# Norm and decay rows of the next block's mixer issued in the out-projection stage of the block before

## Chip, cores and metric

The kernel runs on the eight cores of one Trainium2 chip. Every core runs the same program on one of the eight sequences of the batch, with no exchange between cores. Time is the device time of the slowest core, in microseconds. A core has five instruction streams that run side by side and wait for each other through semaphores: TensorE (PE), VectorE (DVE), ScalarE (ACT), GpSimd (POOL), and SyncE (SP), which here only issues DMAs. Each takes its instructions strictly in order, so an instruction that waits holds up all that stand behind it on its engine.

## What is computed

A Mamba-2 layer and a sliding-window attention layer, each followed by a gated convolutional FFN. The part that the change moves is the start of the Mamba mixer: the normed input `h`, the step sizes `dt`, and what follows from them alone, the running log decay `a_cum` and its exponentials.

```python
h = rms_norm(x, a_norm)
z, xBC, dt = jnp.split(h @ in_proj, [SSM_INNER, SSM_INNER + SSM_CONV_DIM], axis=-1)
xBC = jax.nn.silu(causal_dwconv(xBC, conv_w, conv_b))
dt = jax.nn.softplus(dt + dt_bias);  A = -jnp.exp(A_log)
a = dt * A;  a_cum = jnp.cumsum(a, axis=chunk_position)
seg = a_cum[l] - a_cum[s]                      # decay = exp(seg), causal
y_diag = einsum(cb * decay, x * dt);  states = einsum(B, exp(a_cum[-1] - a_cum), x * dt)
y_off = einsum(C, previous state) * exp(a_cum);  chunk_decay = exp(a_cum[-1])
y = group_rms_norm((y + x * D) * silu(z));     x = x + y @ out_proj
x = x + conv_ffn(x);   x = x + attention(x);   x = x + conv_ffn(x)
```

## The kernel before

The 2048 tokens are cut into four blocks of 512 (b = 0 to 3). Per block there are generators of steps: `mixer_steps(b)`, `mixer_out(b)`, `ffn_steps(b, l)` and `attn_steps(b)`. Each returns a list of (cost, function). `weave` merges lists by the share of their own total cost that each has done, and `FL.run` (lines 1639 to 1647) calls the functions in that order. They run in this sequence:

```python
    FL.run(mixer_steps(0))
    FL.run(mixer_out(0))
    for b in range(NBLK - 1):
        front = ffn_steps(b - 1, 1) if b >= 1 else []
        FL.run(weave(front + ffn_steps(b, 0), mixer_steps(b + 1)))
        FL.run(weave(attn_steps(b), mixer_out(b + 1)))
```

The texts below call the first line M0, the second O0, and the two lines in the loop A1, B1 (b = 0), A2, B2 (b = 1) and A3, B3 (b = 2). In an A stage the FFN of one block shares the engines with the mixer of the next; in a B stage attention of one block shares them with the out-projection of the next.

Calling a function does not emit at once. It records operations; `schedule` (line 432) then places each on its engine. It walks time with a planned cost for each operation and always takes, among those that would be ready, the one recorded first (line 476). A switch of ScalarE's function table weighs 300 places in that choice (line 472). So the order of recording is a priority, not the order of execution: an operation recorded late can be placed early if its inputs and its buffers are free.

`mixer_steps(b)` begins with what the change moves:

- four steps `nrm(t)` of 128 tokens. `tnorm` (line 858) does on ScalarE Square with a row sum, Ln, Exp, and the scaled copy into `sb_Cs`, then eight transposes on TensorE, and on VectorE the product with the gain into `sb_hM`. Its input is `sb_xR` for block 1, and `sb_macc` (filled by a DMA) for blocks 2 and 3. The FFN norms are the same code with `sb_facc` or `sb_fsq` in place of `sb_Cs`, and `sb_hF` in place of `sb_hM`.
- `dt1` (line 938): eight matmuls of 96 output rows with `sb_hM`, then Exp, Ln and the decay scan into `sb_mln`, the write `er_scr` to DRAM and its read `fetch(0)` into `sb_Er`, the Exp and products that make `sb_xtok`, and then the sixteen small float32 matmuls on `sb_cf` with `sb_xtok` and `sb_mln`, whose result VectorE copies to `sb_tokS`.
- `dt3` (line 987): each of two rows is split in three bfloat16 parts on VectorE, written to `al_scr` and `as_scr`, and read back by `rows(0)` as twelve small DMAs into `sb_SR` and `sb_SL`. The segment matmuls (line 366, `sb_SR,sb_SL`) of group 0 need them.
- `dt2` (line 1028): one matmul on `sb_tokS`, then Exp into `sb_cdec`.

After that come eight groups: `inproj(g)` (six chains of eight matmuls with `sb_hM`; conv on ScalarE and VectorE) woven with `ssd(g - 1)`. `fetch` and `rows` are also called by `ssd` for the next group. The weights come through two rings of five slots, `sb_ring_mw` (mixer) and `sb_ring_fw` (FFN, attention). `mixer_out(b)` (line 1229) multiplies `sb_ybuf` by the out-projection: 128 matmuls, in TensorE rows `sb_ring_mw,sb_ybuf`. In O0 it takes turns over all eight banks of PSUM, in B stages over banks 0 and 1.

## Time and profile before

| | |
|---|---|
| median of three runs | 2025.77 us (2016.21, 2025.77, 2180.25) |
| the profiled execution | 2015.09 us; span of its slowest core 2014.0 us |
| spans of the eight cores | 1987.5 to 2014.0 us |
| TensorE matmul busy | 1826.7 us (91%) |
| VectorE, ScalarE busy | 1388.5 us (69%), 1197.6 us (59%) |
| chain that ended last | TensorE 70%, DMA 13%, issue 6%, DVE 5%, ACT 5% |

The table is for core 6, the slowest. The chain is followed back from the last instruction: at each step to what released it. TensorE's matmul time on it says how long the kernel is at least with this order and this clock; what can be taken away lies in the 9% in which TensorE does nothing. The granted clock, averaged over the span, was between 0.975 and 0.981 of full speed on the eight cores. M0 lasts until about 200 us and O0 until 229 us; A1 runs to about 505, B1 to 620, A2 to about 990, B2 to 1100, A3 to about 1465, B3 to about 1580.

### The profile page before, as it was taken

What the parts mean: (1) busy time and instruction counts of PE and PEld (TensorE: products, weight loads), DVE (VectorE), ACT (ScalarE), POOL (GpSimd) and SP (SyncE); (2) the same over time, 40 slices, a digit from 0 to 9 for tenths busy, and PEclk for the clock granted to TensorE, in tenths of its full rate; (3) what the DMA queues carried; (4) which work ended last, traced back from release to release, by engine and by line L of the source; (5) the groups of instructions that cost most, each with busy time, mean ns of one, the idle gap of its engine ahead of it and who ended that gap; (6) DMA issues with size and microseconds to landing.
All of it is one profiled execution on the core that took longest, in us unless ns stands there. A gap on an engine that the chain in (4) does not pass through costs nothing.

```text
span 2014.0 us, 34053 instructions; the slowest of 8 cores (1987.5 to 2014.0 us)
## 1 busy us (share of the span) xinstructions
PE 1826.7 (91%) x9831; PEld 824.7 (41%) x10024; DVE 1388.5 (69%) x2384; ACT 1197.6 (59%) x2144; POOL 259.5 (13%) x434
## 2 busy tenths in 40 slices
PE   4878798999898999899899998899988898999999
PEld 2333443434434444444433443444443344433344
DVE  5898587887757766687675875688676665774362
ACT  3899665756765664565677564576476643665340
POOL 1222111212121111111211111000102000020000
PEclk9999999999898999999999999999999999999999
DMA  7785698999546769999984999944422443433344
GB/s 149 142 169 106 136 196 174 187 181 207 106 130 134 156 142 198 247 227 228 225 233 93 236 222 216 302 160 143 143 83 105 133 153 118 147 115 105 126 148 145
DMA packets 111062, 330.59 MB, mean 164 GB/s; under 512 B 14752, under 2 KB 33312, under 8 KB 110880
## 3 DMA queue, kind: packets, MB, share of 16 engines
q0 software_dynamic: 31392, 113.65, 35.5%
q1 hardware_dynamic: 79488, 214.74, 32.2%
q8 instruction: 86, 1.41, 0.3%
q14 instruction: 96, 0.79, 0.1%
HBM read 375.60 MB, written 66.39 MB: 219 GB/s over the span
## 4 chain that ended last, share of the span: by engine, by line
PE 70%; DMA 13%; issue 6%; DVE 5%; ACT 5%; SPq 0%; POOL 0%; DVEq 0%; ACTq 0%; POOLq 0%
PE ps_ps L353 63%; PE ps_ps L366 5%; DMA w<-sb_ring_fw 4%; DMA sb_ring_fw<-w 2%; DMA sb_ring_mw<-w 2%; PE ps_ps L373 2%; DMA out<-sb_xR 1%; ACT sb_facc L391 1%; DMA sb_Er<-er_scr 1%; DMA sb_xR<-x 1%; DVE sb_macc L417 1%; DMA sb_facc<-pos 1%; ACT sb_macc L391 1%; DVE sb_uF L406 1%; DVE sb_facc L417 1%
## 5 line engine op out<-in xcount | busy, mean ns | idle before, releaser
L353 PE MATMUL ps_ps<-sb_hF,sb_ring_fw 128*128 128x512 bf16 x2394 | 569.4, 381 | 9.9 <-DVE sb_facc L417 2.6
L353 PE MATMUL ps_ps<-sb_hM,sb_ring_mw 128*128 128x512 bf16 (+1 forms) x1525 | 392.3, 393 | 23.5 <-DVE sb_macc L417 10.2
L353 PE MATMUL ps_ps<-sb_ring_fw,sb_uF 128*128 128x512 bf16 (+1 forms) x1650 | 391.3, 376 | 15.9 <-DMA sb_ring_fw<-w 5.6
L353 PEld LDWEIGHTS ps_ps<-sb_hF,sb_ring_fw 128*128 128x128 bf16 x2464 | 235.3, 98 | 281.5 <-issue 21.2
L417 DVE SCALAR_TENSOR_TENSOR sb_facc<-ps_ps,sb_cst,sb_facc 128x511 f32<-128x511 f32 (+2 forms) x400 | 295.6, 744 | 19.2 <-PE ps_ps L353 2.5
L417 DVE SCALAR_TENSOR_TENSOR sb_macc<-ps_ps,sb_cst,sb_macc 128x511 f32<-128x511 f32 (+1 forms) x336 | 248.1, 744 | 13.8 <-DVE sb_facc L406 0.7
L391 ACT ACTIVATE sb_facc<-ps_ps,sb_cst 128x512 f32<-128x512 f32 x213 | 162.6, 766 | 154.8 <-PE ps_ps L353 142.1
L353 PEld LDWEIGHTS ps_ps<-sb_ring_fw,sb_uF 128*128 128x128 bf16 x1696 | 157.6, 98 | 207.4 <-issue 48.9
L353 PEld LDWEIGHTS ps_ps<-sb_hM,sb_ring_mw 128*128 128x128 bf16 (+1 forms) x1568 | 151.7, 101 | 200.9 <-issue 50.1
L406 DVE TENSOR_TENSOR sb_xR<-sb_xR,ps_ps 128x512 f32<-128x512 f32 x128 | 86.3, 683 | 117.2 <-PE ps_ps L353 115.6
L429 POOL DMA_DIRECT2D sb_ring_fw<-w x152 | 83.3, 548 | 634.8 <-PE ps_ps L353 538.6
L406 DVE TENSOR_TENSOR sb_uF<-sb_uF,ps_ps 128x512 bf16<-128x512 bf16 x176 | 118.1, 681 | 68.1 <-PE ps_ps L353 42.6
L353 PE MATMUL ps_ps<-sb_ring_mw,sb_ybuf 128*128 128x512 bf16 (+1 forms) x593 | 148.5, 377 | 7.6 <-DMA sb_ring_mw<-w 2.7
L391 ACT ACTIVATE sb_macc<-ps_ps,sb_cst 128x512 f32<-128x512 f32 x119 | 91.6, 770 | 106.6 <-PE ps_ps L353 99.9
L391 ACT ACTIVATE sb_prevB<-sb_prevF 128x256 bf16<-128x256 f32 x128 | 52.7, 412 | 134.2 <-PE ps_ps L353 49.7
L398 ACT ACTIVATE sb_uF<-sb_facc 128x512 bf16<-128x512 f32 x176 | 96.7, 618 | 24.9 <-DVE sb_facc L417 21.6
L406 POOL TENSOR_TENSOR sb_stmp<-sb_prevF,sb_cdec 128x256 f32<-128x256 f32 x112 | 72.3, 646 | 274.3 <-DVE sb_prevF L406 217.4
L406 DVE TENSOR_TENSOR sb_prevF<-sb_stmp,ps_ps 128x256 f32<-128x256 f32 x112 | 46.5, 415 | 75.8 <-PE ps_ps L353 51.3
L353 PEld LDWEIGHTS ps_ps<-sb_ring_mw,sb_ybuf 128*128 128x128 bf16 x608 | 56.0, 98 | 79.4 <-issue 27.6
L398 ACT ACT_TABLE_LOAD x50 | 64.2, 1283 | 37.7 <-DVE sb_facc L417 24.9
L391 ACT ACT_TABLE_LOAD x54 | 69.3, 1283 | 24.3 <-PE ps_ps L366 16.7
L353 PE MATMUL ps_ps<-sb_hM,sb_ring_fw 128*128 128x512 bf16 x345 | 77.5, 385 | 2.0 <-DVE sb_hM L406 1.6
(219 smaller groups left out, 2315.7 us busy)
## 6 DMA issues: line engine op xcount, KB each, us to landing
sb_ring_fw<-w POOLq DMA_DIRECT2D x152, 512.0 KB, 10.0
sb_ring_fw<-w SPq DMA_DIRECT2D x142, 512.0 KB, 3.6
w<-sb_ring_fw SPq DMA_DIRECT2D x76, 512.0 KB, 14.1
sb_ring_mw<-w SPq DMA_DIRECT2D x74, 512.0 KB, 6.1
sb_ring_mw<-w POOLq DMA_DIRECT2D x64, 512.0 KB, 8.7
w<-sb_ring_mw SPq DMA_DIRECT2D x32, 512.0 KB, 9.4
sb_Er<-er_scr SPq DMA_DIRECT2D x28, 512.0 KB, 11.6
sb_xR<-x SPq DMA_DIRECT2D x16, 512.0 KB, 10.1
```

Source lines behind the costliest of these rows:

```text
L353: return self.add("pe", lambda e: e.matmul(out, lhsT, rhs, start=start, stop=stop), [lhsT, rhs] + ([] if start else [out]), [out], cost=ma ...
L366: ins = e.matmul(out, lhsT, rhs, start=start, stop=stop)
L373: return self.add("pe", lambda e: e.transpose(out, in_, ident), [in_, ident], [out], cost=250.0 if _f32(in_) else 80.0)
L391: return self.add("act", lambda e: e.activation(out, in_, func, **kw), rd, wr, cost=c, tab=TABLE.get(func, 0))
L398: ins = e.activation(out, in_, func)
L406: return self.add(eng, lambda e: e.tensor_tensor(out, in0, in1, op), [in0, in1], [out], cost=c)
L417: return self.add("dve", lambda e: e.scalar_tensor_tensor(out, in0, scalar, in1, op0, op1), rd, [out], cost=190.0 + 1.1 * _n(out))
L429: return self.add(queue, lambda e: e.dma_start(out=out, in_=in_), [in_], [out], dma_sem=sem, cost=900.0 if queue == "pool" else 60.0, lat= ...
```

## The change

The four norm steps, `dt1`, `dt3` and `dt2` leave `mixer_steps` and become a function of their own, `mixer_pre(b, b_in)`. `dt3` follows straight on `dt1` now. For block 0 it runs alone ahead of `mixer_steps(0)`. For block 1 it is woven with `mixer_out(0)`: the transposes and small matmuls use PSUM banks 6 and 7, and the out-projection takes turns over banks 0 to 5 in place of all eight. For blocks 2 and 3 it stands at the end of the list of `mixer_out(1)` and `mixer_out(2)`, on banks 0 and 1, so that it is woven with the last part of attention. `fetch` and `rows` take the block as an argument and do the same as before.

```diff
-    def mixer_steps(b):
+    def mixer_pre(b, b_in):
+
         t0 = b * TB
...
-            bk = b_x() if solo else b_in()
+            bk = b_in()
...
-            fetch(0)
+            fetch(b, 0)
...
-            rows(0)
+            rows(b, 0)
...
         def dt2():
-            bk = b_x() if solo else yb
+            bk = b_in()
...
+        S.append((300.0, dt3))
+        S.append((300.0, dt2))
+        return S
+
+    def mixer_steps(b):
+        t0 = b * TB
+        solo = (b == 0)
...
-                S += weave(inproj(g), ([(1.0, dt3)] if g == 0 else []) + [(800.0, lambda: None)] + side)
+                S += weave(inproj(g), [(800.0, lambda: None)] + side)
...
-        bo = Banks(list(range(8)) if solo else [0, 1])
+        bo = Banks(list(range(6)) if solo else [0, 1])
...
-        return S
+        if solo:
+            return weave(S, mixer_pre(1, Banks([6, 7])))
+        return S + (mixer_pre(b + 1, bo) if b + 1 < NBLK else [])
...
+    FL.run(mixer_pre(0, Banks([0, 1, 2, 3, 4, 5])))
     FL.run(mixer_steps(0))
     FL.run(mixer_out(0))
```

The recorded operations are the same in number and kind; the order on the engines is not. On TensorE, at the end of O0 and the start of A1, the order before was this (`sb_cm` rows are the transposes, with `sb_Cs` those of the mixer's norm, with `sb_facc` and `sb_fsq` those of the FFN's; the 96x512 row is `dt1`):

```order
L353 MATMUL ps_ps<-sb_ring_mw,sb_ybuf 128x512 x66
L373 MATMUL ps_ps<-sb_cm,sb_Cs 128x128 x8
L373 MATMUL ps_ps<-sb_cm,sb_facc 128x128 x8
L373 MATMUL ps_ps<-sb_cm,sb_Cs 128x128 x8
L373 MATMUL ps_ps<-sb_cm,sb_fsq 128x128 x8
L373 MATMUL ps_ps<-sb_cm,sb_Cs 128x128 x8
L373 MATMUL ps_ps<-sb_cm,sb_facc 128x128 x8
L373 MATMUL ps_ps<-sb_cm,sb_Cs 128x128 x8
L373 MATMUL ps_ps<-sb_cm,sb_fsq 128x128 x8
L353 MATMUL ps_ps<-sb_hM,sb_ring_mw 96x512 x8
L353 MATMUL ps_ps<-sb_hF,sb_ring_fw 128x512 x8
```

In the changed kernel the mixer's transposes, `dt1` and the sixteen small matmuls stand ahead, among the out-projection's matmuls; from the last of these small ones on, TensorE has:

```order
L353 MATMUL ps_ps<-sb_cf,sb_mln 128x32
L353 MATMUL ps_ps<-sb_ring_mw,sb_ybuf 128x512 x5
L353 MATMUL ps_ps<-sb_tokS,sb_cf 128x128
L353 MATMUL ps_ps<-sb_hM,sb_ring_mw 128x512 x8
L373 MATMUL ps_ps<-sb_cm,sb_facc 128x128 x8
L373 MATMUL ps_ps<-sb_cm,sb_fsq 128x128 x8
L353 MATMUL ps_ps<-sb_hM,sb_ring_mw 128x512 x8
L373 MATMUL ps_ps<-sb_cm,sb_facc 128x128 x8
L373 MATMUL ps_ps<-sb_cm,sb_fsq 128x128 x8
L353 MATMUL ps_ps<-sb_hM,sb_ring_mw 128x512 x6
L353 MATMUL ps_ps<-sb_hF,sb_ring_fw 128x512 x8
```

So 22 matmuls of the mixer's in-projection (8, 8 and 6) now stand between the last out-projection matmul and the FFN's first, where there were none, and the mixer's 32 transposes and `dt1` are gone from that place.

At the end of B2, still on TensorE, the order before was this (`sb_ring_fw,sb_uF` rows are here attention's output projection, `sb_fsq` the transposes of the FFN's norm that hangs on it):

```order
L373 MATMUL ps_ps<-sb_cm,sb_Cs 128x128 x13
L353 MATMUL ps_ps<-sb_ring_fw,sb_uF 128x512 x12
L373 MATMUL ps_ps<-sb_cm,sb_Cs 128x128 x16
L353 MATMUL ps_ps<-sb_hM,sb_ring_mw 96x512 x2
L373 MATMUL ps_ps<-sb_cm,sb_fsq 128x128 x8
L353 MATMUL ps_ps<-sb_hM,sb_ring_mw 96x512 x6
L353 MATMUL ps_ps<-sb_hF,sb_ring_fw 128x512 x40
L353 MATMUL ps_ps<-sb_hM,sb_ring_mw 128x512 x8
L353 MATMUL ps_ps<-sb_hF,sb_ring_fw 128x512 x2
L353 MATMUL ps_ps<-sb_cf,sb_xtok 128x32
```

And now:

```order
L353 MATMUL ps_ps<-sb_hM,sb_ring_mw 96x512 x3
L353 MATMUL ps_ps<-sb_ring_fw,sb_uF 128x512 x12
L353 MATMUL ps_ps<-sb_cf,sb_xtok 128x32
...
L353 MATMUL ps_ps<-sb_cf,sb_mln 128x32
L353 MATMUL ps_ps<-sb_tokS,sb_cf 128x128
L353 MATMUL ps_ps<-sb_hM,sb_ring_mw 128x512 x4
L373 MATMUL ps_ps<-sb_cm,sb_fsq 128x128 x8
L353 MATMUL ps_ps<-sb_hM,sb_ring_mw 128x512 x12
L353 MATMUL ps_ps<-sb_hF,sb_ring_fw 128x512 x40
```

The small matmuls on `sb_xtok` stood 50 large matmuls behind `dt1`; now they stand 12 behind it, and ahead of the transposes on which the FFN's matmuls hang. At the end of B1 they moved in the same way: eight matmuls of the mixer's first chain and twelve of attention's output stood between, now thirteen of the latter with one attention unit and one set of transposes.

Near the start of the program, on VectorE, one pair changed places. Before:

```order
L421 CAST sb_CBb<-sb_Cs 96x512
L421 CAST sb_Btok<-sb_Wt 96x512
L417 SCALAR_TENSOR_TENSOR sb_CBb<-sb_CBb,sb_cst,sb_Cs 96x512
L421 COPY sb_tokS<-ps_ps 128x256
L417 SCALAR_TENSOR_TENSOR sb_Cs<-sb_Btok,sb_cst,sb_Wt 96x512
```

And now:

```order
L421 CAST sb_CBb<-sb_Cs 96x512
L421 CAST sb_Btok<-sb_Wt 96x512
L421 COPY sb_tokS<-ps_ps 128x256
L417 SCALAR_TENSOR_TENSOR sb_CBb<-sb_CBb,sb_cst,sb_Cs 96x512
L417 SCALAR_TENSOR_TENSOR sb_Cs<-sb_Btok,sb_cst,sb_Wt 96x512
```

The copy to `sb_tokS`, which waits for TensorE's sixteen small matmuls, now stands ahead of the operation that completes `sb_CBb`, which the DMA to `al_scr` takes. Both built programs have 1728 ScalarE operations with a function; where the table that they need changes from one to the next, the order before has 104 switches, and the order now 110: 24 in place of 22 in A2, 26 in place of 22 in A3, and as many as before elsewhere.

## Rows read from the trace of the kernel before

**Rows 1.** The page, busy time of engines: engine, us (share of the span), instructions.
```profile
PE 1826.7 (91%) x9831; PEld 824.7 (41%) x10024; DVE 1388.5 (69%) x2384; ACT 1197.6 (59%) x2144; POOL 259.5 (13%) x434
```

**Rows 2.** Busy time by stretch: stretch, length, engines' busy us, PE clock, DMA share, GB/s.
```profile
75.00:100.00 25.00, 19.78 (x149) 9.63 (x152) 23.82 (x45) 23.24 (x43) 6.80 (x11) 1.00 0.70 120
650.00:675.00 25.00, 24.90 (x119) 11.49 (x119) 18.51 (x33) 15.23 (x30) 3.31 (x6) 1.00 0.84 169
```

**Rows 3.** Timeline of TensorE from the end of O0: start, length, instruction, [idle before].
```profile
223.66 5.34 PE L353 MATMUL ps_ps<-sb_ring_mw,sb_ybuf 128*128 128x512 bf16 x23 [0.17 <-DMA sb_ring_mw<-w]
...
230.76 0.61 PE L373 MATMUL ps_ps<-sb_cm,sb_fsq 128*128 128x128 bf16 x8
234.46 0.61 PE L373 MATMUL ps_ps<-sb_cm,sb_Cs 128*128 128x128 bf16 x8 [3.08 <-ACT sb_Cs L391]
...
239.30 1.01 PE L373 MATMUL ps_ps<-sb_cm,sb_Cs 128*128 128x128 bf16 x8 [3.19 <-ACT sb_Cs L391]
...
241.79 2.66 PE L353 MATMUL ps_ps<-sb_hM,sb_ring_mw 128*96 128x512 bf16 x8 [0.44 <-DVE sb_hM L406]
244.50 1.67 PE L353 MATMUL ps_ps<-sb_hF,sb_ring_fw 128*128 128x512 bf16 x7
```

**Rows 4.** Timeline, same stretch: VectorE's last FFN norm product, ScalarE's part of a conv.
```profile
241.56 1.21 DVE L406 TENSOR_TENSOR sb_hF<-ps_ps,sb_cst 128x1024 bf16<-128x1024 bf16 x1
...
246.27 0.78 ACT L391 ACTIVATE sb_facc<-ps_ps,sb_cst 128x512 f32<-128x512 f32 x1 [0.32 <-PE ps_ps L353]
```

**Rows 5.** TensorE's sixteen small matmuls in A1, first and last of eight rows.
```profile
250.97 0.30 PE L353 MATMUL ps_ps<-sb_cf,sb_xtok 96*128 96x32 f32 x2
...
252.46 0.39 PE L353 MATMUL ps_ps<-sb_cf,sb_mln 96*128 96x32 f32 x2
```

**Rows 6.** Timeline of all engines near the start of the program.
```profile
32.13 0.68 ACT L391 ACTIVATE sb_mln<-ps_ps,sb_cst 96x512 f32<-96x512 f32 x1 [8.05 <-PE ps_ps L353]
...
38.66 0.61 PE L353 MATMUL ps_ps<-sb_cf,sb_xtok 96*128 96x32 f32 x2 [4.25 <-DVE sb_xtok L406]
...
39.11 0.74 DVE L417 SCALAR_TENSOR_TENSOR sb_CBb<-sb_CBb,sb_cst,sb_Cs 96x512 bf16<-96x512 bf16 x1
...
39.92 0.31 SPq L429 DMA_DIRECT2D al_scr<-sb_CBb  x1
...
42.37 0.42 DVE L421 COPY sb_tokS<-ps_ps 128x256 f32<-128x256 f32 x1 [2.52 <-PE ps_ps L353]
...
46.91 3.65 SPq L429 DMA_DIRECT2D sb_SR<-al_scr  x8
...
52.74 3.26 SPq L429 DMA_DIRECT2D sb_SL<-as_scr  x4
...
65.12 0.62 PE L366 MATMUL ps_ps<-sb_SR,sb_SL 47*128 47x512 bf16 x4 [3.43 <-DMA sb_SL<-as_scr]
```

**Rows 7.** Timeline of TensorE and VectorE at the end of B1.
```profile
610.62 1.24 PE L353 MATMUL ps_ps<-sb_hM,sb_ring_mw 128*96 128x512 bf16 x5
...
620.11 1.01 PE L373 MATMUL ps_ps<-sb_cm,sb_fsq 128*128 128x128 bf16 x8 [3.37 <-ACT sb_fsq L391]
...
620.38 0.68 DVE L406 TENSOR_TENSOR sb_xtok<-sb_xtok,sb_Wt 96x512 f32<-96x512 f32 x1
```

**Rows 8.** Timeline of TensorE at the end of B2.
```profile
1096.63 0.61 PE L373 MATMUL ps_ps<-sb_cm,sb_Cs 128*128 128x128 bf16 x8 [0.48 <-ACT sb_Cs L391]
1097.67 0.61 PE L373 MATMUL ps_ps<-sb_cm,sb_Cs 128*128 128x128 bf16 x8 [0.43 <-ACT sb_Cs L391]
1099.84 0.83 PE L353 MATMUL ps_ps<-sb_hM,sb_ring_mw 128*96 128x512 bf16 x2 [1.57 <-DVE sb_hM L406]
```

**Rows 9.** A DMA of A1 and what waited for it: issue on SP, then TensorE.
```profile
322.04 0.41 SPq L429 DMA_DIRECT2D sb_Er<-er_scr  x1
...
341.41 0.59 PE L353 MATMUL ps_ps<-sb_BCb 128*128 128x128 bf16 x4 [7.91 <-DVE sb_prevF L406]
```

**Rows 10.** The page, groups of ScalarE's table loads: count, busy us, mean ns, idle before.
```profile
L391 ACT ACT_TABLE_LOAD x54 | 69.3, 1283 | 24.3 <-PE ps_ps L366 16.7
```

More of the change, by code:

```diff
@@ L978, in toks @@
             def toks():
-                bk = b_x() if solo else b_in()
+                bk = b_in()
                 for t in range(4):
@@ L1124, in post @@
                     if q2 == 1 and g < 7:
-                        fetch(g + 1)
-                        rows(g + 1)
+                        fetch(b, g + 1)
+                        rows(b, g + 1)
                 h["w", q2] = later(1, post)
@@ L1197, in mixer_steps @@
             side = ssd(g - 1) if g >= 1 else []
-            if g == 0:
-                side = [(300.0, dt2)]
             if g >= 2:
```

60 lines of the change are left out of this document (31 added, 29 removed).

## The prediction

> **What bounds the kernel now.** I read the page first: TensorE is busy for 1826.7 of 2014.0 us [rows 1]. At most the rest, 187 us, can be won, and the start of the program, before the first norm is ready, has a good part of it. Then I read the busy time by stretch, which shows two regimes. In M0 VectorE and ScalarE are full (23.82 and 23.24 of 25 us) and TensorE waits for them. In an A stage TensorE is full (24.90 of 25) and ScalarE has room (15.23 of 25) [rows 2]. So a norm that is moved out of an A stage gives nothing where TensorE is full; it gives something only at a boundary between stages. For these I read the timeline.
>
> At the boundary of O0 and A1 the last run of out-projection matmuls ends at 223.66 + 5.34 = 229.00, and the FFN's first matmul starts at 244.50. TensorE waits 3.08 and 3.19 us for ScalarE there, which norms two tiles at a time, one of the mixer and one of the FFN: a pair takes 239.30 - 234.46 = 4.84 us [rows 3]. This is the hole that the change can fill. The ends of B1 and B2 look otherwise. The waits are 3.37 us [rows 7] and 0.48 + 0.43 + 1.57 = 2.48 us [rows 8], and the mixer's norm already lies among attention's last steps there: `schedule` took it early although it was recorded late.
>
> **The change part by part.** No operation is added or removed, so the sum is one of waits.
>
> *O0 and A1.* Into O0 go four sets of transposes (0.61 us each, 2.4), `dt1`'s eight matmuls (at 5.34 / 23 = 0.23 us each, 1.9) [rows 3], and the sixteen small ones with `dt2`'s (252.46 + 0.39 - 250.97 = 1.9 [rows 5], and I add 0.2). The 66 out-projection matmuls stood without a gap, so O0 ends 6.4 us later. Behind it the FFN's last two tiles follow the first two by one ScalarE cycle: the first two's transposes start until 230.76, the next come 4.84 us later, at 235.6, and with 0.61 for them and 1.21 for VectorE's product [rows 3, 4] `sb_hF` is whole at 237.4, 8.4 us after the last out-projection matmul. Two conv operations of ScalarE (0.78 each [rows 4]) now come between, so I take 9.5. The FFN starts at 229.0 + 6.4 + 9.5 = 244.9 in place of 244.50, 0.4 later. But by then 22 in-projection matmuls (5.1 us) and the small ones (2.1) are done, which before came behind 244.50. Net: 7.2 - 0.4 = 6.8 us gained. Bounds: if TensorE waited for nothing there, it would need only the 64 transposes (eight sets at 0.61, 4.9) and `dt1` (1.9) of the 15.5 us, so at most 8.7 are won; if the ScalarE operations of `dt1` (0.68 for the first [rows 6], about five such) still stand ahead of the FFN's norms, 3.4 of it goes: at least 3.4.
>
> *The start.* VectorE's copy to `sb_tokS` waits for TensorE and now stands ahead of the operation that completes `sb_CBb`. That one runs at 42.37 + 0.42 in place of 39.11, 3.7 us later, and so does the DMA to `al_scr` (39.92). SP issued `al_scr`'s reads 7.0 us after the write, at 46.91, and needs 3.65 us for the eight; now it starts at about 50.6 and ends at 54.3, and the four `sb_SL` reads behind them, issued at 52.74, wait until then: 1.5 us late. TensorE already waits 3.43 us for them at 65.12 [rows 6]. M0 runs behind VectorE and ScalarE, which need these matmuls' result, so nothing covers it: 1.5 us lost. Bounds 0 (the order of the conv work around it absorbs it) and 3.7.
>
> *B1 and A2.* The sixteen small matmuls need `sb_xtok`, the end of a chain through ScalarE and VectorE. At the start of the program, with both engines free, it took 38.66 - 32.13 = 6.5 us from `dt1`'s end [rows 6]; at the end of B1, between attention's operations, 620.38 + 0.68 - (610.62 + 1.24) = 9.2 us [rows 7]. I take 8. Behind `dt1` there now stand 13 large matmuls (3.0), one attention unit (0.8) and a set of transposes (0.6): TensorE waits 8 - 4.4 = 3.6 us. Then `dt2`'s matmul waits for the copy (0.42 [rows 6] and the handovers, 0.7), and the FFN's first matmul for the product behind the last transposes (1.21 [rows 4] and a handover, 1.5); two chains of the in-projection stand between and cover the norm. That is 5.8 us in place of 3.37 and some 0.8 of small gaps: 1.6 lost. The out-projection's matmuls now end seven matmuls earlier in attention's list, 1.6 us of TensorE work that no longer fills attention's gaps; I count a fourth of it. Together 2 us lost. Bounds: 3.4 gained, if only the old wait goes and no new one comes, and 6 lost.
>
> *B2 and A3.* Here only the 12 matmuls of attention's output (2.8 us) lie between `dt1` and the small ones. With one more attention operation on ScalarE than at the start the chain takes 7.8: a wait of 5.0, and 0.7 for the copy, against 2.48 before and 0.7 of small gaps. 2.5 lost. The out-projection ends four attention units earlier, 14 matmuls or 3.2 us of cover; half of it, 1.6. Together 4 us lost. Bounds: 3.2 gained, 8 lost. The early small matmuls used to stand 50 matmuls behind `dt1`, where 11.6 us of work hid the chain; this cover is what is gone.
>
> *Table loads.* The order has six more of them, four in A3 and two in A2, each 1.283 us [rows 10], 7.7 us of ScalarE. Both stages leave it 10 of 25 us free [rows 2], so 0 by the row, at most 7.7. The Trainium skill, in ScalarE: Activation LUTs, "Table sets: the hidden batching unit", asks to batch activations by table set; by that rule, taking a block of Exp and Ln out of a stage full of Silu should save loads. The trace agrees on the price of one, and the built order speaks against the saving: 110 switches, not fewer than 104.
>
> *What the DMAs do.* In A1 the whole core stood for 7.91 us behind one `sb_Er` read that was issued at 322.04 and landed about 18 us later [rows 9]. Such a wait depends on what else is queued in that moment. The change shuffles it without aim: 0, bounds 8 either way.
>
> Sum: -6.8 + 1.5 + 2 + 4 = +0.7 us on 2015.1, so 2015.8. This execution is the fastest of the comparable ones; with the 2016.21 and 2025.77 of the table the mean is 2019.0, 3.9 above it. I put the same on the sum: 2019.7.
>
> **The rivals.**
>
> *A, the waits cancel.* Above: 2019.7. For it speaks that at B1 and B2 the norms had already been taken early, so that there the change does little of what it says, and that where it does, TensorE meets a new wait in line.
>
> *B, all boundaries gain.* In-projection matmuls are ready when an A stage starts and fill every hole: 8.7 at A1, the old waits of 3.4 and 3.2 at A2 and A3, nothing lost at the start, and half the `sb_Er` wait (4): 19 us, so 2000. Against it: the small matmuls stand ahead of that filler at A2 and A3, and TensorE can't pass them.
>
> *C, the blocked line costs more.* The wait for `sb_xtok` also delays the FFN norm behind it. ScalarE has to do `dt1`'s chain, and in B1 the Exp of `dt2` too, before the last norm, so that the two waits add instead of overlapping, and TensorE's clock falls: `dt1`'s eight matmuls took 2.66 us (0.33 each) behind the waits of A1, against 0.23 before them [rows 3]. With the upper bounds of both ends (6 + 8), 3.7 at the start and 3.4 at A1: +14, so 2034. It decides from the point where `sb_xtok` is ready more than 10 us after `dt1` in both stages.
>
> *D, ScalarE carries the loads.* [...] As a mechanism here: each of the six loads delays the Silu whose product TensorE needs next, 7.7 us: 2027.4. Only 0.61 of ScalarE's time is taken in A2, which speaks against it.
>
> **How the numbers follow.** A 0.45, B 0.26, C 0.21, D 0.06, something else 0.02. The prediction is A's. Its own range is 2009 to 2030 (the sum's bounds, less the chance that they all fall to one side, and the 10 us by which comparable executions differ). From B to C the range is 1998 to 2040; it leaves out about 2 in 10. A measurement of this kernel can tell about 2%, 40 us, from no change. No case here reaches that: B would need twice its gain, C thrice its loss. Faster by over 2%: 0.01; within 2%: 0.96; slower by over 2%: 0.03.
>
> **What would show it.** In the profile after: between the last out-projection matmul of O0 and the FFN's first, 22 matmuls on `sb_hM` and no wait over 3 us; the `al_scr` write at about 43.5 and the first segment matmuls at about 66.6; a wait for `sb_xtok` of 3 to 5 us ahead of the small matmuls at the end of B1 and of 4 to 6 at the end of B2; 110 table loads. If the waits at `sb_xtok` are under 1 us, B is right. If A1's `sb_Er` wait, or a new one like it, comes or goes by 8 us or more, the sum is wrong for a reason that it doesn't hold.

## The result, and the profile after the change

| | before | after |
|---|---|---|
| median, slowest core | 2020.18 us (14 runs) | 2034.01 us (14 runs) |
| ratio after to before | | 1.0066, 95% interval 1.0047 to 1.0085 |
| profiled execution, span | 2015.09, 2014.0 us | 2026.11, 2025.0 us |
| mean of the eight cores' spans over all comparable runs | 2005.1 us (111 runs) | 2016.0 us (10 runs) |

The change costs 0.66%, 13 us on the slowest core and 11 us on an average core. (The medians are over all 14 runs; the ratio, the last row and everything below leave out the runs in which one half of the chip ran at a lower clock, five of before's and four of after's.) The last row of the table is the finer measure: every run lists the span of each core, the slowest of eight is a matter of luck by some us, and the mean over eight is less so. The text calls it the mean of spans. Its difference is 10.9 ± 2.6 us (95%, as all intervals below). Before's 111 runs are those of the experiments below, on five chips with means of 2004.2 to 2007.0 us, and none ran beside after's ten, which adds a us or two of doubt.

The page after the change (core 1, the slowest), busy time of engines, and the groups of ScalarE's table loads, as [rows 1, 10]:

```profile
PE 1843.3 (91%) x10024; PEld 823.8 (41%) x10024; DVE 1384.8 (68%) x2384; ACT 1208.8 (60%) x2150; POOL 264.8 (13%) x434
...
L391 ACT ACT_TABLE_LOAD x58 | 74.4, 1283 | 25.1 <-PE ps_ps L366 17.0
...
L398 ACT ACT_TABLE_LOAD x52 | 66.7, 1283 | 31.8 <-PE ps_ps L353 18.3
```

Six more instructions on ScalarE, and 58 + 52 = 110 table loads. TensorE's busy times can't be compared between the pages: x9831 before and x10024 now are the same matmuls, with fewer records missing. The two regimes of [rows 2] are as they were, 23.70 and 23.93 us of VectorE and ScalarE in M0, TensorE full in A2:

```profile
75.00:100.00 25.00, 19.59 (x145) 9.18 (x145) 23.70 (x46) 23.93 (x43) 6.17 (x10) 1.00 0.80 142
650.00:675.00 25.00, 25.00 (x126) 11.50 (x124) 20.14 (x37) 12.65 (x26) 2.64 (x5) 1.00 0.89 174
```

**O0 and A1.** TensorE's timeline, as [rows 3]: start, length, instruction, [idle before].

```profile
231.89 0.39 PE L353 MATMUL ps_ps<-sb_tokS,sb_cf 128*128 128x128 f32 x2
232.11 1.89 PE L353 MATMUL ps_ps<-sb_hM,sb_ring_mw 128*128 128x512 bf16 x8
...
236.65 1.89 PE L353 MATMUL ps_ps<-sb_hM,sb_ring_mw 128*128 128x512 bf16 x8 [1.75 <-DVE sb_xR L406]
238.99 0.61 PE L373 MATMUL ps_ps<-sb_cm,sb_facc 128*128 128x128 bf16 x8 [0.45 <-ACT sb_facc L391]
241.18 0.61 PE L373 MATMUL ps_ps<-sb_cm,sb_fsq 128*128 128x128 bf16 x8 [1.59 <-ACT sb_fsq L391]
242.69 1.46 PE L353 MATMUL ps_ps<-sb_hM,sb_ring_mw 128*128 128x512 bf16 x6 [0.91 <-DVE sb_macc L417]
243.98 1.89 PE L353 MATMUL ps_ps<-sb_hF,sb_ring_fw 128*128 128x512 bf16 x8
```

The 22 matmuls on `sb_hM` are there, no wait is over 2 us, and the four waits sum to 4.70 where [rows 3] had 3.08 and 3.19 beside smaller ones. The wait of 1.75 for `sb_xR` comes from the moved steps themselves: VectorE ran the products of `dt3` from 231.75 to 235.9 without a gap, ahead of the `sb_xR` sum at 235.83.

**The start**, all engines, as [rows 6]:

```profile
38.86 0.61 PE L353 MATMUL ps_ps<-sb_cf,sb_xtok 96*128 96x32 f32 x2 [4.90 <-DVE sb_xtok L406]
...
42.56 0.42 DVE L421 COPY sb_tokS<-ps_ps 128x256 f32<-128x256 f32 x1 [3.17 <-PE ps_ps L353]
43.08 0.75 DVE L417 SCALAR_TENSOR_TENSOR sb_CBb<-sb_CBb,sb_cst,sb_Cs 96x512 bf16<-96x512 bf16 x1
...
43.90 0.31 SPq L429 DMA_DIRECT2D al_scr<-sb_CBb  x1
...
48.23 4.08 SPq L429 DMA_DIRECT2D sb_SR<-al_scr  x8
...
52.47 3.27 SPq L429 DMA_DIRECT2D sb_SL<-as_scr  x4
...
61.97 0.39 PE L366 MATMUL ps_ps<-sb_SR,sb_SL 47*128 47x512 bf16 x2
```

The write to `al_scr` is 4.0 us later than before, but its reads are issued 4.3 us behind it in place of 7.0, and the `sb_SL` reads at 52.47, where they were.

**The end of B1**, TensorE, as [rows 7]. The small matmuls wait for nothing; the FFN's transposes and first matmul do:

```profile
615.72 0.61 PE L373 MATMUL ps_ps<-sb_cm,sb_facc 128*128 128x128 bf16 x8 [1.18 <-ACT sb_facc L391]
617.99 2.10 PE L353 MATMUL ps_ps<-sb_ring_fw,sb_uF 128*128 128x512 bf16 x9 [1.66 <-DVE sb_hF L406]
619.93 0.30 PE L353 MATMUL ps_ps<-sb_cf,sb_xtok 96*128 96x32 f32 x2
...
627.81 0.61 PE L373 MATMUL ps_ps<-sb_cm,sb_fsq 128*128 128x128 bf16 x8 [1.39 <-ACT sb_fsq L391]
630.00 10.14 PE L353 MATMUL ps_ps<-sb_hF,sb_ring_fw 128*128 128x512 bf16 x40 [1.58 <-DVE sb_hF L406]
```

**The end of B2**, TensorE, as [rows 8], then four stretches of it by engine (stretch, length, busy of PE, PEld, DVE, ACT, POOL, clock, DMA share, GB/s):

```profile
1100.82 0.38 PE L366 MATMUL ps_ps<-sb_cm 64*128 64x512 bf16 x2
1102.88 0.41 PE L366 MATMUL ps_ps<-sb_facc,sb_vtok 128*64 128x512 bf16 x2 [1.69 <-DVE sb_uF L406]
...
1112.77 2.37 PE L353 MATMUL ps_ps<-sb_ring_fw,sb_uF 128*128 128x512 bf16 x8 [2.80 <-DVE sb_uF L406]
1116.67 0.60 PE L353 MATMUL ps_ps<-sb_cf,sb_xtok 96*128 96x32 f32 x2 [1.54 <-DVE sb_xtok L406]
...
1120.94 0.77 PE L353 MATMUL ps_ps<-sb_tokS,sb_cf 128*128 128x128 f32 x2 [0.68 <-DVE sb_tokS L421]
...
1126.76 8.80 PE L353 MATMUL ps_ps<-sb_hF,sb_ring_fw 128*128 128x512 bf16 x40
```

```profile
1091.00:1106.00 15.00, 12.46 (x104) 5.53 (x100) 10.08 (x12) 14.39 (x24) 0.57 (x1) 1.00 0.34 129
1091.00:1101.00 10.00, 9.59 (x80) 4.12 (x76) 7.49 (x10) 9.39 (x15) 0.00 (x0) 1.00 0.50 191
1101.00:1111.00 10.00, 6.41 (x42) 2.75 (x40) 4.79 (x6) 7.04 (x15) 1.05 (x2) 1.00 0.48 53
1111.00:1126.00 15.00, 11.02 (x47) 7.18 (x48) 11.08 (x21) 7.57 (x17) 2.29 (x4) 0.66 0.96 206
```

TensorE waits more for `sb_uF`, the late products of attention, than for `sb_xtok`. In the last 15 us the granted clock is 0.66 on average, between the levels of 1.2 and 2.4 GHz, behind 10 us in which TensorE was busy for 6.41. The sixteen small matmuls take 3.6 us (1116.67 to 1120.94 - 0.68), where [rows 5] has 1.9. Before has such a fall at this place too, but a shorter one: between the out-projection's end and 12 us into A3 TensorE was busy for 2.9 us per core at the lower level, and in after for 8.9. A matmul takes twice as long there, so this costs 4.5 us in place of 1.5. ScalarE shows why attention is late:

```profile
1101.43 1.04 ACT L391 ACTIVATE sb_facc<-sb_xR 128x1024 bf16<-128x1024 f32 x1
...
1103.16 1.13 ACT L391 ACTIVATE sb_Cs<-sb_macc,sb_nss 128x1024 bf16<-128x1024 f32 x1
1104.20 1.14 ACT L391 ACTIVATE sb_facc<-sb_xR,sb_nss 128x1024 bf16<-128x1024 f32 x1
1105.24 1.00 ACT L391 ACTIVATE sb_facc<-ps_ps 128x1024 bf16<-128x1024 f32 x1
1109.20 0.69 ACT L391 ACTIVATE sb_mln<-ps_ps,sb_cst 96x512 f32<-96x512 f32 x1 [2.96 <-PE ps_ps L353]
1109.79 0.62 ACT L391 ACTIVATE sb_facc<-sb_facc 128x512 f32<-128x512 f32 x1
```

The last scores of attention are ready at 1101.2 (`sb_cm`, 1100.82 + 0.38), and their Exp, `sb_facc<-ps_ps`, runs at 1105.24: ScalarE first does a norm of the FFN (`sb_xR`) and the last of the mixer's (`sb_Cs`). Over the eight cores this delay is 4.0 us, and 1.4 in before, where these norms come later. `dt1`'s Exp (`sb_mln`) stands ahead of attention's two `sb_facc<-sb_facc` as well, but its idle 2.96 us cost attention little: their input, VectorE's sum with `sb_esink`, is itself ready only at 1109.20 (1108.51 + 0.69), so they come 0.6 us later by the Exp, and the second one another 0.5 by the Ln behind it. e4 below has attention's operation ahead of `dt1`'s Exp and still 4.0 us of waits for `sb_uF` per core, against 4.9 here. Nor is it that ScalarE is full: 14.39 of 15 us here, and before has a stretch with 14.2.

**Stage by stage.** From the timelines of all eight cores I took the times of the same marks, and subtracted the TensorE work ahead of each in the built order (0.213 us for a matmul of 512 columns, the cost that the steps' lists use), so that work done earlier or later doesn't count. Mean of eight cores, us more than before; the standard error (not the 95% interval) is 1.6 to 2.1 in M0, 0.3 to 0.9 at the boundaries, 1.4 to 2.8 in the A stages. Counting the small float32 matmuls at their measured 0.11 us and setting the end marks of the A stages otherwise moves the boundary rows by up to 0.9 us at A1 and A3 and up to 2 at A2. The stretch behind A3 has no row.

| | after | e1 | e2 | e3 | e4 | e7 | e15 |
|---|---|---|---|---|---|---|---|
| M0, to its last state matmul | +6.2 | +5.9 | +3.3 | +2.1 | +2.2 | +1.1 | +3.8 |
| to the FFN's first matmul in A1 | -3.6 | +0.8 | -3.1 | +0.1 | +0.1 | 0.0 | -3.3 |
| rest of A1 | 0.0 | +3.7 | +5.1 | +0.3 | +3.0 | +4.4 | -5.1 |
| B1, to the first in A2 | +1.0 | +0.8 | +0.4 | +1.0 | +0.2 | +2.5 | +0.7 |
| rest of A2 | -1.9 | +1.9 | +1.6 | -2.4 | +0.2 | +1.5 | +1.0 |
| B2, to the first in A3 | +10.4 | +0.4 | -0.6 | +1.7 | +6.4 | -0.6 | -0.9 |
| rest of A3 | -2.7 | +1.2 | -0.3 | -0.4 | -4.0 | +6.5 | +0.5 |
| whole execution | +8.2 | +14.6 | +6.6 | +4.5 | +8.7 | +14.8 | -2.0 |

The profiled execution of before is a short one: its mean of spans is 1999.9, 5.2 below the mean of its runs. So every column has some 5 us too much, in M0 and A1 (e2, e3, e4 and e7 have M0 in before's order and still show +1.1 to +3.3; e1, e3, e4 and e7 have A1 in before's order and show +0.3 to +4.4). Totals are therefore taken from the runs, and of this table only the boundaries.

For M0 the kept traces give a better comparison. Eleven kernels have VectorE's order of before up to the end of O0, and two, after and e1, have the new one. The new ones reach their first segment matmul 0.2 us sooner, at 155 us they are level, and their last state matmul comes 4.4 us later, at 209.5 in place of 205.1; the standard errors are 0.5 to 0.6. So M0's loss appears in its last 50 us, and not at the start.

### The profile page after: what moved, and what is told of

Read it like the earlier page. It is cut to its first block, busy times and chain, and to the rows that moved or that the text cites. A ratio compares the mean times of both kernels' runs of the same rounds, so it can differ in the third digit from the quotient of the medians.

```text
span 2025.0 us, 34178 instructions; the slowest of 8 cores (1990.6 to 2025.0 us)
## 1 busy us (share of the span) xinstructions
PE 1843.3 (91%) x10024; PEld 823.8 (41%) x10024; DVE 1384.8 (68%) x2384; ACT 1208.8 (60%) x2150; POOL 264.8 (13%) x434
## 4 chain that ended last, share of the span: by engine, by line
PE 70%; DMA 13%; ACT 6%; issue 5%; DVE 5%; POOL 0%; SPq 0%; DVEq 0%; ACTq 0%; POOLq 0%
PE ps_ps L353 63%; PE ps_ps L366 5%; DMA w<-sb_ring_fw 4%; DMA sb_ring_fw<-w 3%; PE ps_ps L373 2%; DMA sb_Er<-er_scr 2%; ACT sb_facc L391 1%; DMA sb_facc<-pos 1%; DMA sb_xR<-x 1%; DMA out<-sb_xR 1%; DVE sb_uF L406 1%; DVE sb_macc L417 1%; DMA sb_ring_mw<-w 1%; DVE sb_facc L417 1%; ACT sb_macc L391 1%
## 5 line engine op out<-in xcount | busy, mean ns | idle before, releaser
L353 PE MATMUL ps_ps<-sb_hF,sb_ring_fw 128*128 128x512 bf16 x2464 | 577.5, 382 | 4.2 <-DVE sb_hF L406 2.9
L353 PE MATMUL ps_ps<-sb_hM,sb_ring_mw 128*128 128x512 bf16 (+1 forms) x1568 | 391.0, 386 | 26.6 <-DVE sb_macc L417 11.9
L353 PE MATMUL ps_ps<-sb_ring_fw,sb_uF 128*128 128x512 bf16 (+1 forms) x1696 | 395.4, 377 | 18.8 <-DVE sb_uF L406 8.8
## 6 DMA issues: line engine op xcount, KB each, us to landing
sb_ring_fw<-w POOLq DMA_DIRECT2D x152, 512.0 KB, 10.4
sb_xR<-x SPq DMA_DIRECT2D x16, 512.0 KB, 11.4
```

Source lines behind the costliest of these rows:

```text
L353: return self.add("pe", lambda e: e.matmul(out, lhsT, rhs, start=start, stop=stop), [lhsT, rhs] + ([] if start else [out]), [out], cost=ma ...
```

## The experiments

All are against the runs of before on the same chip. The table gives the ratio on the slowest core with its 95% interval, and the difference in the mean of spans with a 95% interval. The expectations quote such differences against all runs of before that there were by then, so theirs differ from the table's by some tenths of a us.

| | ratio, slowest core | mean of spans, us |
|---|---|---|
| e1 block 0 alone | 1.0043 (1.0023, 1.0064) | +5.7 ± 2.9 |
| e2 block 1 alone | 1.0013 (0.9995, 1.0032) | -0.1 ± 2.0 |
| e3 block 2 alone | 1.0045 (1.0026, 1.0064) | +2.1 ± 2.7 |
| e4 block 3 alone | 1.0022 (0.9998, 1.0047) | +3.7 ± 2.2 |
| e5 e1, banks of before | 0.9996 (0.9979, 1.0013) | -0.3 ± 2.7 |
| e6 e4, split | 1.0016 (0.9998, 1.0035) | +4.0 ± 2.4 |
| e7 e4, appended | 1.0044 (1.0027, 1.0061) | +8.9 ± 2.1 |
| e8 whole change, banks as e5 | 1.0046 (1.0029, 1.0063) | +7.7 ± 2.1 |
| e9 before, `sb_Er` on ScalarE's queue | 1.0007 (0.9991, 1.0023) | +2.2 ± 1.6 |
| e10 e2, same | 0.9994 (0.9978, 1.0010) | -0.8 ± 2.5 |
| e11 e7, late rows | 1.0024 (1.0007, 1.0042) | +4.2 ± 2.2 |
| e12 e11, paced | 1.0017 (1.0002, 1.0032) | +1.0 ± 1.9 |
| e13 e4, paced | 1.0034 (1.0017, 1.0052) | +6.5 ± 2.0 |
| e14 e8, paced | 1.0028 (1.0009, 1.0046) | +1.6 ± 2.4 |
| e15 e2, paced | 0.9981 (0.9950, 1.0012) | -5.5 ± 2.3 |
| e16 e15 again | 0.9982 (0.9947, 1.0017) | -2.9 ± 5.5 |
| e17 e3, paced | 1.0027 (0.9999, 1.0054) | +3.2 ± 2.5 |

**One block at a time (e1 to e4).** A tuple says of which blocks the steps stay in `mixer_steps`, at the place, on the banks and in the weave of before:

```diff
+IN = (False, True, True, True)
...
+        if IN[b]:
+            S = mixer_pre(b, b_in, b_x if solo else b_in, b_x if solo else Banks([yb]))
+            S, dt3, dt2 = S[:5], [(1.0, S[5][1])], S[6:]
```

e1 has False for block 0 alone, e2, e3 and e4 for block 1, 2 and 3.

> The kernel before with one part of the change: for block 0 alone the norm and decay steps are a list of their own ahead of the mixer's groups; blocks 1 to 3 stand as before. The order differs from before in M0 only. Theory (the loss has two seats, M0 and the boundary of B2 and A3): the first segment matmuls come at the same time as before, but M0, which runs behind VectorE and ScalarE, ends about 6 us later, since its operations are dealt in another order; 6 us slower than before, ratio about 1.003. Rival (the change has no seat of its own; any new order moves the time by what the reads into sb_Er happen to do): within 2 us of before, and if not, then through an sb_Er wait in A1. My step of the prediction: 1.5 us slower, through the copy to sb_tokS.

> The kernel before with one part of the change: the norm and decay steps of block 1 alone are woven with the out-projection of block 0 (banks 6 and 7; the out-projection has banks 0 to 5). The order differs at O0 and the start of A1 only. Theory: the boundary gives 3.6 us, the time from the last state matmul of M0 to the FFN's first matmul less the work in it, ratio about 0.998. The prediction's step: 6.8 us faster. Rival: 0, since the out-projection's matmuls were needed to fill the end of M0 and now the transposes take their place there.

> The kernel before with one part of the change: the norm and decay steps of block 2 alone stand behind the out-projection in B1. The order differs at the end of B1 and the start of A2 only. Theory: 1 us slower, ratio 1.0005, which can't be told from no change; the wait for sb_xtok is under 1 us here because 13 large matmuls and an attention unit cover it. Rival (the blocked line costs in B1 as in B2): 8 us slower or more.

> The kernel before with one part of the change: the norm and decay steps of block 3 alone stand behind the out-projection in B2. The order differs at the end of B2 and the start of A3 only. Theory: the boundary costs about 10 us (waits of some 8 us for sb_uF and sb_xtok in place of 3.2, and the matmuls around them at the lower clock), of which A3 gives back about 3: 8 us slower, ratio 1.004. Rival (scatter): within 2 us of before.

The means of spans add up: 5.7 - 0.1 + 2.1 + 3.7 = 11.4, known to about 5, and the whole change has 10.9 (2016.0 - 2005.1). So the loss sits in blocks 0 and 3, perhaps some in block 2 (2.1 ± 2.7), and block 1 gives nothing although its boundary gains 3.1 us. No loss at all is out for block 0 (5.7 ± 2.9) and block 3 (3.7 ± 2.2). Of the expectations e1's theory came true in size, e2's did not (3.6 gained was expected), e3's did in the mean, and e4's 3.7 lies between its theory (8) and its rival (2). On the slowest core e3 costs more, 7.9 ± 3.0 us, as neighbouring cores lie further apart in it:

```profile
core 0: 1997.5 us, clock 0.981
core 1: 2016.6 us, clock 0.975
core 2: 1981.7 us, clock 0.981
core 3: 2011.6 us, clock 0.979
```

Over its seven runs the cores 0 and 1, 2 and 3 and so on differ by 26.0 us, against 14.4 in before's.

**Block 0's banks (e5, e8).**

```diff
-        FL.run(mixer_pre(0, Banks([0, 1, 2, 3, 4, 5])))
+        FL.run(mixer_pre(0, Banks([0, 1, 2]), Banks([3, 4, 5, 6]), Banks([5])))
...
+        if solo:
+            b_x.n = 3
+            b_in.n = 4
```

> The kernel of e1 (block 0's norm and decay steps in a list of their own, all else as before), but these steps take the PSUM banks that they took before: the transposes banks 0 to 2, the decay matmuls 3 to 6, the last one 5, and the groups go on in the rotation where it stood before. The order of ScalarE, GpSimd and SP is then that of before but for a few rows, and VectorE's copy to sb_tokS still stands ahead. e1 was slower by 0.43%, 8.8 us on the slowest core and 5.8 us in the mean of all cores' spans. Theory (M0's loss comes from the banks, which decide when a product may be placed and so deal the whole of M0 anew): within 2 us of before in the mean of spans. Rival (the early copy and the early decay rows cost it): still 4 us or more slower.

> The whole change, with block 0's banks kept as in e5. If the parts add up (means of spans against before: e5 0, e2 -0.1, e3 +2.2, e4 +3.8), it is 6 us above before in the mean of spans, where the whole change was 11.2 above, and about 2025 on the slowest core. Rival (block 0's part costs only through what follows it): no better than the whole change, 2031 or more.

With the banks of before e1's loss is gone. But e5 does not do what its expectation says: in its trace the copy to `sb_tokS` is back behind the operation that completes `sb_CBb`, and VectorE's order is that of before in all 2384 places, where e1's differs in 133, all between 40 and 195 us. So e5 shows that the list of its own costs nothing and the banks decide the order; it can't tell the early copy from the rest of the new order, since both went together. The traces do that: where the copy is early, the first segment matmuls are not late, and the 4.4 us come at the end of M0 (above). So block 0's part costs through the rotation of banks. That it does so because later products of M0 found their banks free at other times, and the planner dealt M0 anew in a stage that VectorE and ScalarE bound, is the reading of the planner's code; which of the new places costs was not tried. e8, the whole change with the banks of before, is 3.2 ± 3.4 us below the whole change by the means, which agrees and shows nothing by itself. The sum of parts said +5.5 for it (5.7 left out of 11.4, e5's -0.3 in its place), and 7.7 ± 2.1 doesn't contradict that.

**Where block 3's steps stand (e6, e7).** e6 leaves the norm and the chain up to `sb_xtok` in B2 and puts the rest at the start of A3. In it, by the code, the last small matmul writes a bank whose in-projection product has not been read yet, so that its output isn't the reference's; the work is the same. e7 records the steps behind the woven list:

```diff
-        FL.run(weave(attn_steps(b), mixer_out(b + 1)))
+        FL.run(weave(attn_steps(b), mixer_out(b + 1)) + pre.get(b + 2, []))
```

> The kernel of e4 (block 3 alone moved), but the sixteen small matmuls on sb_xtok, the split rows and the last small matmul stand at the start of A3 again; only the norm and the decay chain up to sb_xtok stay in B2. Eight in-projection matmuls now stand ahead of the small ones. In e4 TensorE waited between the out-projection's end in B2 and the FFN's first matmul 4.0 us for sb_uF, 2.1 for sb_xtok and 0.7 for sb_tokS. Theory (ScalarE is full in B2's last stretch, 14.4 of 15 us, and the early norm and decay chain push attention's last Exps back): the waits for sb_xtok and sb_tokS go, that for sb_uF stays at 3 us or more, and the mean of spans stays 2 to 4 us above before (e4: 3.8). Rival (the blocked line, as I had it in the prediction): the loss goes, within 1 us of before.

> The kernel of e4 (block 3 alone moved), but its norm and decay steps are recorded behind the woven list of attention and out-projection instead of at the end of the out-projection's own list: they still stand ahead of A3, but attention comes first on ScalarE and the out-projection ends as late as before. Theory (the place among attention costs, not the place ahead of the FFN): the waits between the out-projection's end and the FFN's first matmul fall from 6.9 to about 3.5 us as before, mean of spans within 1.5 us of before. Rival (ahead of the FFN's norm is what costs): 3 us or more above before.

By the timelines of all eight cores, in e6 the waits between the out-projection's end and the FFN's first matmul are 2.8 us per core for `sb_uF`, 1.4 for `sb_xtok` and 0.7 for `sb_tokS`, against 4.0, 2.1 and 0.7 in e4: the last two did not go, since the eight in-projection matmuls cover only a part, and the time stays at +4.0. Neither theory is confirmed by it in full; the small matmuls' place ahead of the FFN's norm as the whole cause is out. In e7 TensorE's end of B2 is before's again:

```profile
1104.42 1.06 PE L353 MATMUL ps_ps<-sb_hM,sb_ring_mw 128*96 128x512 bf16 x2 [1.57 <-DVE sb_hM L406]
...
1108.27 7.07 PE L353 MATMUL ps_ps<-sb_hF,sb_ring_fw 128*128 128x512 bf16 x32
```

The 1.57 is that of [rows 8], the boundary costs -0.6 in place of +6.4, and yet the kernel is 8.9 us slower, the most of all single parts. So the theory is right on the boundary and the rival on the time, and the stage table puts the loss in A3, +6.5 with a standard error of 2.2.

The boundary of e4 can be added up from the traces of all cores: its waits between the out-projection's end and the FFN's first matmul are 6.9 us in place of 3.3, and the time that TensorE works at the lower clock costs 4.4 in place of 1.5. Together that is 6.5, and the stage table has 6.4. In e7 both are near those of before (3.3 and 2.3). So close to half of the boundary's price is the clock. The delay between attention's last scores and their Exp is 4.8 us in e4 and 1.4 in e7 as in before. In e6 it is 1.3, and the waits for `sb_uF` are there all the same, so this delay is not the whole reason for them.

**The `sb_Er` read (e9, e10).**

```diff
-        o = K.dma("sp", bufs(b, g, "Er"), er_d[b % 2]...
+        o = K.dma("act" if b == 1 else "sp", bufs(b, g, "Er"), er_d[b % 2]...
```

> The kernel before with one edit that the change does not have: in A1 the eight reads into sb_Er are issued by ScalarE's DMA queue instead of SP's, where they stand behind the writes of 512 KB from the rings. TensorE's order is the same. In the traces whose block 1 stands as before TensorE waited 7.4 to 10.0 us per core between 325 and 390 us behind such a read. Theory (the read waits in SP's queue): the wait falls below 4 us and the mean of spans by 4 us or more against before. Rival (in A1 the 16 DMA engines are busy the whole time, 0.94 to 1.05 of a stretch, whoever issues): the wait stays at 7 us or more and the mean within 2 us of before.

> e2 (block 1 alone moved into O0) with the same edit of the sb_Er reads as e9. In e2 the boundary of O0 and A1 gave 3 to 4.5 us, the mean of spans did not move (-0.1), and the wait behind sb_Er was 11.3 us per core, 3 more than where block 1 stands as before. Theory (the gain is given back at this read, which lands when the DMA engines are through, not when TensorE comes): if e9 takes the wait away, this kernel is 3 us or more below e9 in the mean of spans; if e9 does not take it away, the two are equal again and the wait is again 3 us longer here. Rival (the gain is lost elsewhere, in the FFN's start or at the lower clock): equal to e9 although the wait is gone.

For e9 the rival holds on the wait, 10.4 us, and its 2.2 ± 1.6 us lie at the rival's bound. The page's table of issues (KB each, median us to landing; the first row is that of the other three blocks) and TensorE's row in A1:

```profile
sb_Er<-er_scr SPq DMA_DIRECT2D x20, 512.0 KB, 10.9
sb_Er<-er_scr ACTq DMA_DIRECT2D x8, 512.0 KB, 17.7
```

```profile
340.54 0.58 PE L353 MATMUL ps_ps<-sb_BCb 128*128 128x128 bf16 x4 [10.42 <-DVE sb_prevF L406]
```

On a queue of their own the reads are no faster. Against the same eight reads of A1 in before, whose medians were 9.5 to 13.5 us by core, they are slower: 14.1 to 17.7. e10 is 3.0 ± 3.0 us below e9, as the theory says for a wait that is gone; but the wait was not gone (7.5 us per core in A1 for `sb_prevF`, 10.4 in e9), so neither branch of the theory came true. And over the whole of A1 the kernels with block 1 in its old place have 7.1 to 13.1 us of it, so that e2's 12.2 stands out from nothing. That the gain of block 1 is eaten by this read was argued, and isn't shown. What is in e2's A1 and not in before's is a wait for `sb_prevB`, 1.7 us per core. (A new wait for `sb_hF`, 2.4, stands ahead of the FFN's first matmul, and the boundary's 3.1 already counts it.) Where the gain went stays open: the rest of A1 reads +5.1 in e2, but up to +4.4 in kernels whose A1 is before's.

**The pace of what stays (e11 to e17).** The steps that left `mixer_steps` had a cost of 4 x 600 + 1800 in its list, and `weave` deals by shares of a list's cost. e11 is e7 with `dt3` and `dt2` back in A3's first group. "Paced" puts in their place

```diff
+            S = S + [(600.0, lambda: None)] * 4 + [(1800.0, lambda: None)]
```

> e7 (block 3's norm and decay steps behind the woven list of B2) with one thing put back: the split rows and the last small matmul stand in A3's first group again, as before. e7 had the waits at the end of B2 as before (3.3 against 3.5 us) and yet was 8.6 us above before in the mean of spans; its A3 was 6.5 us longer by the trace. Theory (the early split rows and last small matmul deal the products of A3's first groups anew, as the banks did in M0): within 2 us of before. Rival (any list ahead of A3 costs the same, since it is the norm's place ahead of the FFN's that counts): 6 us or more above before again.

> e11 with five empty steps of the costs of the moved ones (four of 600, one of 1800) at the head of the mixer's list in A3, where the norm and decay steps stood. The empty steps issue nothing; they give the weave of A3 the shares that it had before. e11 was 4.3 us above before in the mean of spans, all of it in A3, and there TensorE's order ran the in-projection earlier. Theory (what leaves a woven list changes the pace of what stays in it: the in-projection comes earlier and the FFN, whose weights come by DMA, later): within 1.5 us of before. Rival (the mixer's norm recorded ahead of the FFN's costs, whatever the pace): 4 us above before as e11.

> e4 (block 3 alone moved, in the place of the change) with the same five empty steps at the head of A3's mixer list. e4 was 3.8 us above before in the mean of spans: its boundary of B2 and A3 cost 5 to 6 us by the trace. Theory (the boundary's waits for sb_uF are the cost here; the pace comes on top): 2 to 5 us above before. Rival (the pace was all of it): within 1 us of before.

> The whole change with block 0's banks kept as in e5 and the five empty steps at the head of the mixer's list in A1, A2 and A3. e8 (banks alone) was 7.3 us above before in the mean of spans. Theory: the pace gives 2 us or more of that back, so 5 us or less above before. Rival: as e8.

> e2 (block 1 alone moved) with the five empty steps at the head of A1's mixer list: the version that the runs so far point to. Theory (the boundary's 3 to 4.5 us are real, and e2 lost them to the pace of A1 and to the sb_Er read): 2 us or more below before in the mean of spans. Rival (the sb_Er read in A1 takes them whatever the pace): within 1 us of before, as e2.

e7 to e11 to e12: +8.9, +4.2, +1.0, steps of 4.7 ± 3.1 and 3.2 ± 2.9. All three have the norms ahead of A3 and outside attention; the first step puts the split rows back, the second, which issues no instruction, the pace. So e7's loss is the order of A3, about half by the early rows, half by the pace. (In the second step ScalarE's order also loses four table loads, 104 as in before where e4, e7 and e11 have 108, and the runs can't tell these from the pace.) A norm ahead of the FFN's costs little: 1.0 ± 1.9 in the mean of spans, 0.17% (0.02 to 0.32) on the slowest core. In the whole change the pace is worth 6.1 ± 3.2 us (e8 +7.7, e14 +1.6), and with banks and pace as before it is not to be told from before in the mean of spans; on the slowest core it is still 0.28% slower (0.09 to 0.46), and its boundary at B2 still costs 6.9 us by the trace. For block 3 in the change's own place the pace did not help: e13 +6.5 against e4 +3.7, above its theory's 2 to 5, with the boundary at 6.7, where e4 has 6.4. There the cost is the boundary, and whether e4's A3 really gave 4.0 back through its pace stays open. So what the pace gives in the whole change is, as far as the single parts show, A1's.

For block 1 it turned the sign. A1's waits of TensorE, on the slowest core of e2 and then of e15 (total us, times, longest):

```profile
PE ps_ps L353 <- DVE sb_prevF L406: 9.9, 1, 9.9
```

```profile
PE ps_ps L353 <- DVE sb_macc L417: 18.2, 2, 13.5
```

Core 1 of e15 has its wait under another name; over the eight cores `sb_prevF` fell from 12.2 to 0.2 us each, `sb_macc` rose from 2.9 to 5.9, and all waits between 250 and 490 us together fell from 19.4 to 12.7, where kernels with A1 in before's order have 15.0 to 19.4. The reads into `sb_Er` are no faster: their medians in A1 are 12.3 to 14.9 us by core, against 10.1 to 14.1 in e2. The wait for `sb_prevF` is at 0.2 in e14 and e16 too, the other two with block 1 moved and paced, and on each of their cores; it is 7.1 us or more in every other kernel. So it is the order that A1 gets from the two together that leaves these reads time. How much of e15's gain is this and how much the boundary was not tried apart.

> e15 once more, on another chip: block 1 alone moved into O0, A1 paced as before. e15 was 5.5 us below before in the mean of spans, with a ratio of 0.9981 (0.9950 to 1.0012) on the slowest core. If it is real: again 3 us or more below in the mean of spans, ratio 0.997 to 0.999. Rival (chance, or that chip): within 2 us.

> e3 (block 2 alone moved) with the five empty steps at the head of A2's mixer list. e3 was 2.2 us above before in the mean of spans and 7.9 on the slowest core, with the two cores of a pair 26 us apart where before has 15. Theory (A2's new pace set its DMA waits and drew the pairs apart): within 1.5 us in the mean and pairs 15 to 18 us apart. Rival (the boundary's order does it): as e3.

e16 by itself, -2.9 ± 5.5, decides between its expectation and chance no more than it denies e15. Both together, weighted by their intervals: 5.1 ± 2.1 us below before in the mean of spans, and 0.9981 (0.9958 to 1.0005) on the slowest core. That beats the changed kernel clearly, and before on an average core; on the slowest core it is not settled. e17 leaves e3's puzzle open: the mean did not fall (+3.2), the pairs are 19.4 us apart in place of 26.0, with 16.1 in before's runs on the same chip. The paced parts add up to -0.3 (e5) - 5.1 + 3.2 + 6.5 = +4.3, and e14 has +1.6 ± 2.4.

## The prediction, step by step

**Failed: "M0" was left out of the sum.** The prediction priced the start by one pair of VectorE's that changed places, 1.5 us through `sb_SL`, and took the rest of M0 as untouched. Block 0's part cost 5.7 ± 2.9 us, gone with the banks of before (e5), and by the traces it appears at the end of M0. The order of the two built programs showed M0 reshuffled; I had read it at the first rows only. The 1.5 itself failed too: the write to `al_scr` came at 43.90, as worked out (43.5), but its reads came 4.3 us behind it and not 7.0, and the first segment matmuls at 61.97 and not 66.6. The 7.0 of [rows 6] had slack in it.

**Mis-sized: O0 and A1.** -6.8 in the sum. The 22 matmuls and the absence of long waits came as said. From O0's last `sb_tokS` matmul to the FFN's first it was 243.98 - 232.1 = 11.9 us, not 9.5, since beside ScalarE's two conv operations TensorE also waited for VectorE's `sb_xR`, which stood behind the products of `dt3`, and `sb_macc` (1.75 and 0.91). The boundary gave 3.6 us (e2: 3.1), near the lower bound, and in the runs e2 gave 0.1. The step that failed is the belief that a gain at the boundary is a gain of the kernel: e2 with A1's new pace had none of it, e15 with the old pace 5.5. Where e2 lost it isn't shown.

**Right in size, wrong in place: B1 and A2.** +2 in the sum, +1.0 in the trace, 2.1 ± 2.7 in e3. No wait for `sb_xtok` at all, where 3.6 was forecast; the waits stood before the FFN's norm, 1.18 + 1.66 + 1.39 + 1.58 = 5.8, by accident the 5.8 of the prediction. The slowest core's 7.9 us are in no step of it.

**Mis-sized: B2 and A3.** +4 in the sum, upper bound 8; 10.4 in the trace of after, 6.4 in e4's, 3.7 ± 2.2 in e4's runs. The wait for `sb_xtok` was 1.54 and that for `sb_tokS` 0.68, against 5.0 and 0.7. What took their place is attention, 4.9 us per core for `sb_uF` in after and 4.0 in e4, and the clock: 8.9 us of TensorE's work at the lower level in place of 2.9, some 3 us that the sum had at nothing. I had named a blocked line on TensorE; on ScalarE, which I had left out, the mixer's and the FFN's norms stand ahead of attention's last Exp and it comes 4.0 us behind its scores in place of 1.4. e6 says that this is not all. The cover that is gone (1.6) was the right idea at too low a price; e7, where the out-projection ends as late as before, has no boundary loss.

**Right as far as tried: table loads.** 110, as said. Their cost was not tried by itself, and rival D, 7.7 us, is bounded only: e1 loses its 5.7 with before's 104 loads, e14 has all 110 and +1.6 ± 2.4. But e3 has two more than before, e4 four, and e12, which is level with before, none more, so a part of the losses of blocks 2 and 3 may be theirs.

**Half right: the `sb_Er` reads.** The prediction gave them 0 ± 8 and no aim. In after core 1 had two such waits of 8 us; the first, with the issue of the read on SP and VectorE's product that needed it:

```profile
266.15 0.37 SPq L429 DMA_DIRECT2D sb_Er<-er_scr  x1
...
302.07 0.69 DVE L406 TENSOR_TENSOR sb_Cs<-sb_Er,sb_BCb 128x1024 bf16<-128x1024 bf16 x1 [12.67 <-DMA sb_Er<-er_scr]
...
303.83 0.59 PE L353 MATMUL ps_ps<-sb_BCb 128*128 128x128 bf16 x4 [8.05 <-DVE sb_prevF L406]
```

This read took 35.8 us from issue to landing, where the median of the eight in A1 is 14.3. Per core the sum of the waits between 250 and 490 us is 8.2, against 8.1 before, so they do not carry the loss. But that they can't be steered was wrong: with block 1 moved and the pace kept they fall to 0.2.

**The cases.** Time and sign were rival C's (2034; its terms on 2019.0 give 2033.3, since 2019.7 already holds the sum's 0.7). Its mechanism was so in part. Its clock did fall in B2, and its A1 term, 3.4 gained, is what the boundary gave. But `sb_xtok` was ready 6.4 us after `dt1` in B1 and 8.0 in B2, and not more than 10, its start term did not occur, and M0's banks and A1's pace, which made up most of the loss, were in no rival. Case A failed because its terms priced only what stands near a moved step. 2034.0 lies outside A's own range of 2009 to 2030, and inside the wide one from B to C for other reasons than that was drawn for.
